# First attention of a two-block kernel: 1/sum carried by a diagonal matrix instead of a scaling pass

## The chip, the cores and the metric
The program runs on one NeuronCore of a Trainium2 chip. Its engines work side by side, each through its own list of instructions in order: PE (TensorE, matrix products), DVE (VectorE), ACT (ScalarE), POOL (GpSimd) and SP (which only issues transfers here). They wait for one another through semaphores. The metric is the device time of one execution in microseconds (us); lower is better.

## The reference
Two transformer blocks run one after the other over 256 tokens of width 1024, in float32. The first has an attention (8 query heads of 64, 2 key/value heads, 512 keys: 256 of a context and 256 of the tokens) and beside it a gated linear recurrence; the second has two further attentions and an MLP. The change touches the first attention alone:

```
def latent_attention(qx, kx, vx, kc, vc):
    ...
    scale = ATT_HEAD_DIM ** -0.5
    def block(q):
        s = jnp.einsum('bqkgd,bnkd->bkgqn', q, keys).astype(jnp.float32) * scale
        p = jax.nn.softmax(s, axis=-1)
        return jnp.einsum('bkgqn,bnkd->bqkgd', p.astype(vals.dtype), vals)
```

with q = rope(rmsnorm(q) * g_q) and k = rope(rmsnorm(k) * g_k). Softmax is exp(s - max) divided by its sum over the 512 keys.

## The kernel before, in words
Nothing is scheduled by a planner: each engine's list is written out by hand, and the order in the source is the order on the engine. `Steps` counts what an engine has finished under a name; `tick` raises the count, `done` raises it and makes DVE wait for it, and `wait_ge(..., DV["probs 3"])` makes another engine wait for that step.

The first attention is cut into 16 units n (8 heads x 2 blocks of 128 queries). Each unit has five steps:

- PE `scores n`: one matmul, 64 x 128 queries against 512 keys, into bank n % 2.
- DVE `max n`: a maximum over the 512 scores (L1227), and a tiny operation that multiplies it by -1/8 (L1228). The result is the bias of the exponential.
- ACT `exp n` (L744): exp(score/8 + bias) from the bank into `probs`, with the row sum beside it.
- DVE `probs n`: the reciprocal of the sum (L1209) and a multiplication of all 512 columns by it (L1210).
- PE `pT n` (L1659): four 128x128 transposes of `probs` into bank 2 + n % 2; ACT copies them out (L736). For every second unit PE then multiplies the transposed probabilities of a head (two units) by the values: `values h`, four matmuls.

The orders around it. PE: `scores n+1`, a piece of the recurrence (`hg_tail n`), `pT n`, and after even n from 2 on `values n/2-1`. The tails are 8 transposes at n = 1, 8 matmuls at n = 2 and 3, 16 matmuls at n = 4 and 5 (8 each in float32 of 256 columns), one of 512 columns at n = 7 and 8, and 8 one-column matmuls at n = 9; n = 6 and 10 to 15 have none. DVE: `probs n-1`, `max n`, then `acc`, a multiply-add over 1024 columns that reduces the modulation weights and has nothing to do with the attention (L1096), and at n = 11 `hg_out`, a block of five operations that finishes the recurrence (L1217 to L1221). ACT: `exp n`, the copy of `pT n-1`, its own tails; at n = 8 these hold a table load, a logarithm and the load back before `exp 9`. From n = 13 ACT also makes the high halves of the next weights, and POOL the low halves (L558).

After unit 15 PE does `values 7`, a reduction (`mod 3`), and then the output projection, which runs back to back.

Of the kernel before, what the change touches and what calls it, by code (L numbers as in the profile page):

```python
# [24 lines left out]
ALU = mybir.AluOpType  # L25
ACT = mybir.ActivationFunctionType
AX = mybir.AxisListType.X

P = 128
# [3 lines left out]
HD = 64  # L33
# [63 lines left out]
class Steps:  # L97
# [8 lines left out]
    def tick(self, name):  # L106
        assert name not in self.seen, name
        self.seen.append(name)
        self.n += 1
        if self.order is not None:  # L110
            assert self.order[self.n - 1] == name, (name, self.order[self.n - 1])
        return 1
# [7 lines left out]
def program(nc, a, out, orders):  # L120

    ctx = ExitStack()
    with ctx:
# [6 lines left out]
        ps = [ctx.enter_context(nc.psum_tensor(f"bank{i}", [P, 512], F32)) for i in range(8)]  # L130
# [11 lines left out]
        stat = sb("stat", [P, 256])  # L142
# [4 lines left out]
        dg = sb("rstd_diag", [P, 2, P])  # L147
        rby = sb("rstd_b", [P, T])
        ident = cst[:, C_ID:C_ID + P]
# [17 lines left out]
        kv = sb("kv", [P, 4, 256], F32, b1)  # L167
        qk = sb("q_k", [P, 2, 640], F32, b1)
        gqk = sb("g_qk_b", [P, 640], F32, b1)
# [31 lines left out]
        pr = sb("probs", [P, 2, 512], F32, r)  # L201
# [154 lines left out]
        PE, AC, DV, PL = (Steps(sem(f"{n}_step"), orders and orders[n]) for n in ("pe", "act", "dve", "pool"))  # L356
# [255 lines left out]
        def _(act):  # L612
# [31 lines left out]
            for t in range(4):  # L644
                src = x[:, t, :] if t < 2 else cx[:, t - 2, :]
                if t:
                    act.wait_ge(AC.sem, AC[f"sq {t - 1}"])
                nc.scalar.activation(junk, src, ACT.Square,
                                     accum_out=stat[:, 64 + t:65 + t]).then_inc(AC.sem, AC.tick(f"sq {t}"))
# [90 lines left out]
            for n in range(16):  # L740
                act.wait_ge(DV.sem, DV[f"max {n}"])
                if n >= 2:
                    act.wait_ge(PE.sem, PE[f"pT {n - 2}"])
                nc.scalar.activation(pr[:, n % 2, :], ps[n % 2][:], ACT.Exp, bias=stat[:, 128 + n:129 + n],  # L744
                                     scale=HD ** -0.5, accum_out=stat[:, 144 + n:145 + n]).then_inc(AC.sem, AC.tick(f"exp {n}"))
                if n >= 1:
                    probs_by_key(n - 1)
                hg_tail(n)
                if n >= 13:
                    hi(W_END["g"] + n - 12)  # L750
# [34 lines left out]
            with act.Fori(0, MLP1_TRIPS) as i:  # L785
                for v in range(2):
                    g = 1 + v
# [94 lines left out]
            for n in range(17):  # L882
                if n < 16:
                    scale = HD ** -0.5 if n < 8 else 96 ** -0.5
# [3 lines left out]
                    for t, (c0, c1) in enumerate(((0, P), (P, 384))):  # L888
                        nc.scalar.activation(pc[:, n % 2, c0:c1], ps[n % 2][:, c0:c1], ACT.Exp, bias=stat[:, 128 + 2 * n + t:129 + 2 * n + t],
                                             scale=scale, accum_out=stat[:, 160 + 2 * n + t:161 + 2 * n + t]  # L890
                                             ).then_inc(AC.sem, AC.tick(f"cexp {n} {t}"))
                if n % 4 == 3:
                    g = n // 4
# [84 lines left out]
        def _(dve):  # L978
            V = nc.vector
# [5 lines left out]
            def tick(ins, name):  # L985
                ins.then_inc(DV.sem, DV.tick(name))

            def done(ins, name):
                ins.then_inc(DV.sem, DV.tick(name))
                dve.wait_ge(DV.sem, DV[name])  # L990
# [162 lines left out]
            for l, n in enumerate(LEVELS):  # L1153
                for i in range(2):
                    dve.wait_ge(PE.sem, PE[f"level {l} {i}"])
                    own(f"at diag {i}" if l == 0 else f"at {l - 1} {i}")
                    mask = cst[:, C_LVL + P * l:C_LVL + P * l + P].bitcast(U32).unsqueeze(1).broadcast_to([P, HG, P])
                    tick(V.copy_predicated(at[:, i, :, P * i:P * i + P], mask,
                                           ps[6 + i][:].rearrange("p (h t) -> p h t", h=HG)), f"at {l} {i}")
                grow(n)  # L1160
                if n == 4:

                    dve.wait_ge(AC.sem, AC["kv 1"])
                    tick(V.tensor_copy(qk[:, :, 512:640], kv[:, 0:2, 0:P]), "k in")
                if n == 16:

                    dve.wait_ge(AC.sem, AC["q 1"])
                    own("k in")
                    V.tensor_tensor(tmp2[:, :, 0:P], kv[:, 2:4, 0:P], kv[:, 2:4, 0:P], ALU.mult)
                    done(V.tensor_tensor(tmp[:], qk[:], qk[:], ALU.mult), "qk sq")  # L1170
                    V.tensor_reduce(stat[:, 80:100].rearrange("p (t h) -> p t h", t=2), tmp[:].rearrange("p t (h d) -> p t h d", d=HD), AX, ALU.add)
                    tick(V.tensor_reduce(stat[:, 100:104].rearrange("p (t h) -> p t h", t=2),
                                         tmp2[:, :, 0:P].rearrange("p t (h d) -> p t h d", d=HD), AX, ALU.add), "qk ss")
                if n == 32:
                    dve.wait_ge(AC.sem, AC["rstd qk"])
                    dve.wait_ge(s_bc, 160)
                    qk4 = qk[:].rearrange("p t (h d) -> p t h d", d=HD)
                    kc4 = kv[:, 2:4, 0:P].rearrange("p t (h d) -> p t h d", d=HD)
                    V.tensor_tensor(qk4, qk4, stat[:, 104:124].rearrange("p (t h) -> p t h", t=2).unsqueeze(3).broadcast_to([P, 2, 10, HD]), ALU.mult)
                    done(V.tensor_tensor(kc4, kc4, stat[:, 124:128].rearrange("p (t h) -> p t h", t=2).unsqueeze(3).broadcast_to([P, 2, 2, HD]), ALU.mult), "qk n")  # L1180
                    V.tensor_tensor(kv[:, 2:4, 0:P], kv[:, 2:4, 0:P], gqk[:, 512:640].unsqueeze(1).broadcast_to([P, 2, P]), ALU.mult)
                    done(V.tensor_tensor(qk[:], qk[:], gqk[:].unsqueeze(1).broadcast_to([P, 2, 640]), ALU.mult), "qk g")
                if n == 64:

                    for t in range(2):
                        c4 = cst[:, C_COS + HD * t:C_COS + HD * t + HD].unsqueeze(1).broadcast_to([P, 10, HD])
                        V.tensor_tensor(tmp[:, t, :].rearrange("p (h d) -> p h d", d=HD), qk4[:, t], c4, ALU.mult)
                        x5 = qk[:, t, :].rearrange("p (h a two i) -> p h a two i", a=2, two=2, i=16)
                        o5 = tmp2[:, t, :].rearrange("p (h a two i) -> p h a two i", a=2, two=2, i=16)
                        s5 = cst[:, C_SIN + HD * t:C_SIN + HD * t + HD].rearrange("p (a two i) -> p a two i", a=2, two=2)  # L1190
                        for half in range(2):
                            ins = V.tensor_tensor(o5[:, :, :, half, :], x5[:, :, :, 1 - half, :],
                                                  s5[:, :, half, :].unsqueeze(1).broadcast_to([P, 10, 2, 16]), ALU.mult)
                    done(ins, "rope")
                    done(V.tensor_tensor(qk[:], tmp[:], tmp2[:], ALU.add), "qk")
# [11 lines left out]
            def probs(n):  # L1207
                dve.wait_ge(AC.sem, AC[f"exp {n}"])
                done(V.reciprocal(stat[:, 160 + n:161 + n], stat[:, 144 + n:145 + n]), f"sum {n}")  # L1209
                tick(V.tensor_scalar(pr[:, n % 2, :], pr[:, n % 2, :], stat[:, 160 + n:161 + n], None, ALU.mult), f"probs {n}")  # L1210

            def hg_out():

# [7 lines left out]
                tick(V.tensor_tensor(flat(cl, 4, 4), xn[:, 1, :], flat(ch, 4, 4).bitcast(F32), ALU.subtract), "cat lo")  # L1221

            for n in range(16):
                if n >= 1:
                    probs(n - 1)
                dve.wait_ge(PE.sem, PE[f"scores {n}"])
                done(V.tensor_reduce(stat[:, 128 + n:129 + n], ps[n % 2][:], AX, ALU.max), f"m {n}")  # L1227
                done(V.tensor_scalar(stat[:, 128 + n:129 + n], stat[:, 128 + n:129 + n], -HD ** -0.5, None, ALU.mult), f"max {n}")  # L1228
                acc(2 + n // KT, n % KT)
                if n == 11:  # L1230
                    hg_out()
                if n == 10:

                    dve.wait_ge(PE.sem, PE["mod 2"])
                    done(V.tensor_tensor(mod2[:, 8:16], ps[5][:, 0:8], cols[:, R_BMOD + 32:R_BMOD + 40], ALU.add), "mod2 s")
                    tick(V.scalar_tensor_tensor(out=mod2[:, 8:16], in0=mod2[:, 8:16], scalar=1.0, in1=cols[:, R_G2:R_G2 + 8],
                                                op0=ALU.add, op1=ALU.mult), "mod2 scale")
# [215 lines left out]
        def _(pe):  # L1453
            def mm(out_, l, r_, start, stop=True):
                return nc.tensor.matmul(out_, l, r_, start=start, stop=stop, skip_group_check=True)  # L1455
# [196 lines left out]
            def probs_t(n):  # L1652
                pe.wait_ge(DV.sem, DV[f"probs {n}"])
                if n >= 2:
                    pe.wait_ge(AC.sem, AC[f"pT {n - 2}"])
                else:
                    pe.wait_ge(AC.sem, AC["qT 2"])
                for k in range(4):
                    ins = nc.tensor.transpose(ps[2 + n % 2][:, P * k:P * k + P], pr[:, n % 2, P * k:P * k + P], ident)  # L1659
                ins.then_inc(PE.sem, PE.tick(f"pT {n}"))  # L1660

            def values(h):
# [364 lines left out]
```

## Time and profile before

| | us |
|---|---|
| median of 3 executions | 999.83 |
| the three executions | 995.11, 999.83, 1000.09 |
| span of the profiled execution (first to last instruction) | 991.5 |
| the profiled execution's own time | not listed apart from the three |
| PE busy | 891.4 (90%) |
| DVE busy | 464.1 (47%) |
| ACT busy | 409.5 (41%) |
| POOL busy | 461.2 (47%) |
| mean granted clock of TensorE | 0.941 of full |

The units of the attention lie between 237 and 316 us of the span. A row of the timeline gives start, length, engine, line, operation, output and inputs, and in brackets the idle time of the engine before it and what ended that. Matmuls overlap in the record, so what one costs is read from its start to the start of the next, not from its length. A float32 matmul leaves two records, a transpose one: "x16" under a matmul of the recurrence is 8 matmuls, "x4" under L1659 is 4 transposes. A granted clock of 1.00 is 2.4 GHz and 0.50 is 1.2 GHz.

### The profile page before, as it was taken

How to read it: one execution, taken by the hardware profiler on the slowest of the kernel's cores; microseconds unless marked ns; L12 is line 12 of the kernel's file. 1: busy time of each engine (PE TensorE's matmuls, PEld its weight loads, DVE VectorE, ACT ScalarE, POOL GpSimd, SP SyncE). 2: the span in 40 equal slices, each digit the busy share in tenths (PEclk: the TensorE clock that was granted, in tenths of full speed). 3: DMA queues.
4: the chain of work that ended last, by engine and by line, in shares of the span. 5: the costliest groups of instructions: out<-in, count | busy, mean ns of one | idle time of the engine just before them, and what ended most of it. 6: DMA issues, size and time to landing. Idle time of an engine off the chain costs nothing.

```text
span 991.5 us, 13660 instructions
## 1 busy us (share of the span) xinstructions
PE 891.4 (90%) x5233; PEld 740.5 (75%) x5233; DVE 464.1 (47%) x642; ACT 409.5 (41%) x627; POOL 461.2 (47%) x225
## 2 busy tenths in 40 slices
PE   5599997997988889999999699999998599999995
PEld 0157797786644669999998587877797489999994
DVE  0259856698574262333333605353325643334334
ACT  1232321215353443444435464544473534444443
POOL 4053634310003616474756398543375356564653
PEclk9799997899977989999999699999999789999998
DMA  9957841221344416656564277432344335666541
GB/s 198 270 198 237 278 122 45 84 64 52 104 121 150 128 64 181 201 170 196 172 201 137 82 217 178 141 86 85 107 137 140 106 89 189 190 189 191 178 161 42
DMA packets 89290, 145.76 MB, mean 147 GB/s; under 512 B 15260, under 2 KB 55297, under 8 KB 89249
## 3 DMA queue, kind: packets, MB, share of 16 engines
q1 hardware_dynamic: 88112, 143.23, 46.6%
q0 software_dynamic: 1104, 1.96, 1.8%
q8 instruction: 27, 0.44, 0.2%
q14 instruction: 15, 0.11, 0.0%
q10 hardware_dynamic: 32, 0.01, 0.0%
HBM read 144.13 MB, written 1.05 MB: 146 GB/s over the span
## 4 chain that ended last, share of the span: by engine, by line
PE 73%; DVE 13%; issue 5%; ACT 3%; DMA 3%; POOL 2%; SPq 0%; DVEq 0%; ACTq 0%; POOLq 0%
PE bank L1455 71%; DMA raw<-in_w_mod 3%; POOL w_lo L558 1%; ACT w_hi L620 1%; DVE hg_kb L1149 1%; DVE hg_b L1151 1%; DVE mod_acc L1096 1%; POOL z_lo L594 1%; PE bank L1659 1%; PE bank L1935 1%; DVE probs L1210 1%; DVE hg_kf L1149 1%; DVE yn L1419 1%; DVE merged_lo L1406 1%; DVE hg_f L1151 0%
## 5 line engine op out<-in xcount | busy, mean ns | idle before, releaser
L558 POOL TENSOR_TENSOR w_lo<-raw,w_hi 128x1024 fp32r<-128x1024 f32 (+2 forms) x177 | 431.6, 2451 | 488.3 <-ACT w_hi L620 446.4
L620 ACT ACTIVATE w_hi<-raw 128x1024 fp32r<-128x1024 f32 (+1 forms) x218 | 227.3, 1044 | 258.0 <-PE bank L1455 243.5
L1455 PE MATMUL bank<-z_hi,w_hi 128*128 128x256 f32 x384 | 111.8, 291 | 2.4 <-POOL z_lo L594 2.4
L1455 PE MATMUL bank<-z_lo,w_hi 128*128 128x256 f32 x384 | 110.3, 287 | 0.0
L1455 PE MATMUL bank<-z_hi,w_lo 128*128 128x256 f32 x384 | 110.1, 287 | 0.0
L1007 DVE TENSOR_TENSOR w_lo<-raw,w_hi 128x1024 fp32r<-128x1024 f32 x44 | 57.4, 1315 | 112.6 <-ACT w_hi L620 112.6
L1455 PE MATMUL bank<-n_hi,w_hi 128*128 128x256 f32 x352 | 100.8, 286 | 1.4 <-DVE w_lo L1007 0.5
L1455 PE MATMUL bank<-n_lo,w_hi 128*128 128x256 f32 x352 | 99.9, 284 | 0.0
L1455 PE MATMUL bank<-n_hi,w_lo 128*128 128x256 f32 x352 | 99.8, 284 | 0.0
L1455 PE MATMUL bank<-w_hi,mlp_h_hi 128*128 128x512 f32 x216 | 84.9, 393 | 3.0 <-DVE mlp_h_lo L1441 1.5
L1455 PE MATMUL bank<-w_lo,mlp_h_hi 128*128 128x512 f32 x216 | 84.7, 392 | 0.0
L1455 PE MATMUL bank<-w_hi,mlp_h_lo 128*128 128x512 f32 x216 | 84.5, 391 | 0.0
L1455 PEld LDWEIGHTS bank<-z_hi,w_hi 128*128 128x128 f32 x384 | 75.3, 196 | 5.2 <-issue 3.1
L1455 PEld LDWEIGHTS bank<-z_lo,w_hi 128*128 128x128 f32 x384 | 75.4, 196 | 0.6
L1455 PEld LDWEIGHTS bank<-z_hi,w_lo 128*128 128x128 f32 x384 | 75.3, 196 | 0.0
L1455 PEld LDWEIGHTS bank<-n_hi,w_hi 128*128 128x128 f32 x352 | 67.2, 191 | 3.6 <-POOL w_lo L558 1.3
L1455 PEld LDWEIGHTS bank<-n_lo,w_hi 128*128 128x128 f32 x352 | 67.3, 191 | 0.4
L1455 PEld LDWEIGHTS bank<-n_hi,w_lo 128*128 128x128 f32 x352 | 67.1, 191 | 0.0
L1455 PEld LDWEIGHTS bank<-w_hi,mlp_h_hi 128*128 128x128 f32 x216 | 40.7, 188 | 11.8 <-DVE mlp_h_lo L1441 1.9
L1439 DVE TENSOR_TENSOR mlp_h<-mlp_relu 128x512 f32<-128x512 f32 x16 | 11.1, 693 | 81.4 <-ACT mlp_relu L958 81.4
L1455 PE MATMUL bank<-raw,c_silu 128*2 128x512 f32 x64 | 32.3, 658 | 17.7 <-DMA raw<-in_w_mod 17.7
L1455 PEld LDWEIGHTS bank<-w_hi,mlp_h_lo 128*128 128x128 f32 x216 | 40.6, 188 | 8.9
(355 smaller groups left out, 1783.3 us busy)
## 6 DMA issues: line engine op xcount, KB each, us to landing
raw<-in_w_in SPq DMA_DIRECT2D x54, 512.0 KB, 4.3
raw<-in_w_down SPq DMA_DIRECT2D x54, 512.0 KB, 3.6
raw<-in_w_mod SPq DMA_DIRECT2D x48, 512.0 KB, 4.3
raw<-in_w_gu SPq DMA_DIRECT2D x44, 512.0 KB, 3.5
raw<-in_w_up SPq DMA_DIRECT2D x32, 512.0 KB, 3.6
raw<-in_w_out SPq DMA_DIRECT2D x12, 512.0 KB, 3.6
raw<-in_w_in SPq DMA_DIRECT2D x8, 336.0 KB, 3.0
raw<-in_w_out SPq DMA_DIRECT2D x8, 256.0 KB, 3.7
```

The costliest lines, as they stand in the source:

```text
L558: nc.gpsimd.tensor_tensor(wl[:, w % SPL, 0:size], raw[:, slot_raw, 0:size], wh[:, w % SPL, 0:size].bitcast(F32), ALU.subtract).then_inc(s_ ...
L594: nc.gpsimd.tensor_tensor(zl[:, k, :], zf[:, k % 4, :], zh[:, k, :].bitcast(F32), ALU.subtract).then_inc(PL.sem, PL.tick(f"{name}l {k}"))
L620: nc.scalar.activation(wh[:, w % SPL, 0:size], raw[:, slot_raw, 0:size], ACT.Copy).then_inc(s_hi, 1)
L1007: V.tensor_tensor(wl[:, w % SPL, :], raw[:, slot_raw, :], wh[:, w % SPL, :].bitcast(F32), ALU.subtract).then_inc(s_lod, 1)
L1096: ins = V.scalar_tensor_tensor(out=to, in0=raw[:, n % RAW, :], scalar=csil[:, k, 0:1], in1=to, op0=ALU.mult, op1=ALU.add)
L1149: ins = V.tensor_tensor(kv_[:, :, 1 - fwd, :], kv_[:, :, 1 - fwd, :], tot(fwd), ALU.mult)
L1151: done(V.tensor_tensor(fv[:, :, 0, 0:1], fv[:, :, 0, 0:1], fv[:, :, 1, 0:1], ALU.mult), f"total {n} {fwd}")
L1210: tick(V.tensor_scalar(pr[:, n % 2, :], pr[:, n % 2, :], stat[:, 160 + n:161 + n], None, ALU.mult), f"probs {n}")
L1406: tick(V.tensor_tensor(flat(mgl, k0, n), flat(mgf, k0, n), flat(mgh, k0, n).bitcast(F32), ALU.subtract), f"merged lo {b}")
L1419: ins = V.scalar_tensor_tensor(out=yn[:, t, 512 * j:512 * j + 512], in0=ps[bank + 2 * t + j][:], scalar=stat[:, 216 + t:217 + t], in1=gpos ...
L1439: V.tensor_tensor(h2[:, g % 3, :], rr[:, g % 3, :], rr[:, g % 3, :], ALU.mult).then_inc(s_h2, 1)
L1455: return nc.tensor.matmul(out_, l, r_, start=start, stop=stop, skip_group_check=True)
```

## The change
The division by the row sum is no longer a pass over the probabilities. DVE multiplies the 128x128 identity by the reciprocal, which gives a diagonal matrix in `dg` (128 columns instead of 512), and PE's four transposes become four ordinary float32 matmuls of `probs` with that diagonal: they transpose and scale at once. The factor 1/8 moves from the exponential and the maximum into g_q: the gain multiplication of queries and keys is split in two, and the one of the queries has the factor in it. The maximum is written negated by the reduction itself, so that L1228 goes, and DVE no longer waits for its own result there. Last, on DVE `max n` now stands ahead of `probs n-1`.

```
-                                     scale=HD ** -0.5, accum_out=stat[:, 144 + n:145 + n]).then_inc(AC.sem, AC.tick(f"exp {n}"))
+                                     accum_out=stat[:, 144 + n:145 + n]).then_inc(AC.sem, AC.tick(f"exp {n}"))
...
-                    V.tensor_tensor(kv[:, 2:4, 0:P], kv[:, 2:4, 0:P], gqk[:, 512:640].unsqueeze(1).broadcast_to([P, 2, P]), ALU.mult)
-                    done(V.tensor_tensor(qk[:], qk[:], gqk[:].unsqueeze(1).broadcast_to([P, 2, 640]), ALU.mult), "qk g")
+                    kg = gqk[:, 512:640].unsqueeze(1).broadcast_to([P, 2, P])
+                    V.tensor_tensor(kv[:, 2:4, 0:P], kv[:, 2:4, 0:P], kg, ALU.mult)
+                    V.tensor_tensor(qk[:, :, 512:640], qk[:, :, 512:640], kg, ALU.mult)
+                    done(V.scalar_tensor_tensor(out=qk[:, :, 0:512], in0=qk[:, :, 0:512], scalar=HD ** -0.5,
+                                                in1=gqk[:, 0:512].unsqueeze(1).broadcast_to([P, 2, 512]),
+                                                op0=ALU.mult, op1=ALU.mult), "qk g")
...
-                tick(V.tensor_scalar(pr[:, n % 2, :], pr[:, n % 2, :], stat[:, 160 + n:161 + n], None, ALU.mult), f"probs {n}")
+                tick(V.tensor_scalar(dg[:, n % 2, :], ident, stat[:, 160 + n:161 + n], None, ALU.mult), f"probs {n}")
...
             for n in range(16):
+                dve.wait_ge(PE.sem, PE[f"scores {n}"])
+                tick(V.tensor_reduce(stat[:, 128 + n:129 + n], ps[n % 2][:], AX, ALU.max, negate=True), f"max {n}")
                 if n >= 1:
                     probs(n - 1)
-                dve.wait_ge(PE.sem, PE[f"scores {n}"])
-                done(V.tensor_reduce(stat[:, 128 + n:129 + n], ps[n % 2][:], AX, ALU.max), f"m {n}")
-                done(V.tensor_scalar(stat[:, 128 + n:129 + n], stat[:, 128 + n:129 + n], -HD ** -0.5, None, ALU.mult), f"max {n}")
                 acc(2 + n // KT, n % KT)
...
-                    ins = nc.tensor.transpose(ps[2 + n % 2][:, P * k:P * k + P], pr[:, n % 2, P * k:P * k + P], ident)
+                    ins = mm(ps[2 + n % 2][:, P * k:P * k + P], pr[:, n % 2, P * k:P * k + P], dg[:, n % 2, :], True)
```

DVE's list at the start of units 13 and 14, before. The reciprocal and `probs` (L1209, L1210) of the last unit come first, then the maximum of this one:

```order
L1209 RECIPROCAL stat<-stat 128x1 [waits act_step]
L1210 TENSOR_SCALAR probs<-probs,stat 128x512 [waits dve_step]
L1227 TENSOR_REDUCE stat<-bank 128x1 [waits pe_step]
L1228 TENSOR_SCALAR stat<-stat 128x1 [waits dve_step]
L1096 SCALAR_TENSOR_TENSOR mod_acc<-raw,c_silu,mod_acc 128x1024 [waits acc_used,raw_full5,dve_step]
L1209 RECIPROCAL stat<-stat 128x1 [waits act_step]
L1210 TENSOR_SCALAR probs<-probs,stat 128x512 [waits dve_step]
L1227 TENSOR_REDUCE stat<-bank 128x1 [waits pe_step]
L1228 TENSOR_SCALAR stat<-stat 128x1 [waits dve_step]
```

The same place after the change (`rstd_diag` is the name of `dg`; the lines are 4 higher, or 2 for the maximum):

```order
L1229 TENSOR_REDUCE stat<-bank 128x1 [waits pe_step]
L1213 RECIPROCAL stat<-stat 128x1 [waits act_step]
L1214 TENSOR_SCALAR rstd_diag<-cst,stat 128x128 [waits dve_step]
L1096 SCALAR_TENSOR_TENSOR mod_acc<-raw,c_silu,mod_acc 128x1024 [waits acc_used,raw_full5]
L1229 TENSOR_REDUCE stat<-bank 128x1 [waits pe_step]
L1213 RECIPROCAL stat<-stat 128x1 [waits act_step]
L1214 TENSOR_SCALAR rstd_diag<-cst,stat 128x128 [waits dve_step]
```

The maximum, which waits for PE, has moved ahead of the reciprocal and the diagonal of the unit before; four operations are left where there were five.

PE's list at units 10 to 12, before: `scores n+1` (keysT,qT), then the transposes of unit n, then in even units the values:

```order
L1455 MATMUL bank<-keysT,qT 128x512 [waits act_step]
L1659 MATMUL bank<-cst,probs 128x128 [waits act_step,dve_step]
L1659 MATMUL bank<-cst,probs 128x128 x3
L1455 MATMUL bank<-probsT,kv 64x256 [waits dve_step,act_step]
L1455 MATMUL bank<-probsT,kv 64x256 x3
L1455 MATMUL bank<-keysT,qT 128x512 [waits act_step]
L1659 MATMUL bank<-cst,probs 128x128 [waits act_step,dve_step]
```

And after:

```order
L1458 MATMUL bank<-keysT,qT 128x512 [waits act_step]
L1458 MATMUL bank<-rstd_diag,probs 128x128 [waits act_step,dve_step]
L1458 MATMUL bank<-rstd_diag,probs 128x128 x3
L1458 MATMUL bank<-probsT,kv 64x256 [waits dve_step,act_step]
L1458 MATMUL bank<-probsT,kv 64x256 x3
L1458 MATMUL bank<-keysT,qT 128x512 [waits act_step]
L1458 MATMUL bank<-rstd_diag,probs 128x128 [waits act_step,dve_step]
```

Nothing has moved on PE; the four transposes have become four matmuls with the diagonal. ACT's list is the same.

## Rows read from the trace of the kernel before

**Rows 1.** The page, the chain that ended last: shares of the span by engine.

```profile
PE 73%; DVE 13%; issue 5%; ACT 3%; DMA 3%; POOL 2%; SPq 0%; DVEq 0%; ACTq 0%; POOLq 0%
```

**Rows 2.** Stretches: from:to, length, busy time of each engine (records), PE clock, DMA.

```profile
237.00:270.00 33.00, 29.90 (x135) 19.59 (x136) 19.63 (x39) 13.22 (x30) 0.00 (x0) 0.95 0.38 112
270.00:282.00 12.00, 11.28 (x50) 5.97 (x48) 6.46 (x14) 8.51 (x15) 0.00 (x0) 1.00 0.46 133
282.00:316.00 34.00, 26.67 (x71) 12.64 (x72) 24.22 (x38) 12.73 (x25) 7.84 (x4) 0.67 0.50 152
```

**Rows 3.** Timeline of PE in unit 3 (start, length, line, tiles).

```profile
252.08 2.05 PE L1455 MATMUL bank<-hg_v,hg_k_tok 128*128 128x128 f32 x16
253.97 0.60 PE L1659 MATMUL bank<-cst,probs 128*128 128x128 f32 x4
254.50 1.12 PE L1455 MATMUL bank<-keysT,qT 64*128 64x512 f32 x2
```

**Rows 4.** Timeline of PE in units 5 to 7.

```profile
266.12 0.60 PE L1659 MATMUL bank<-cst,probs 128*128 128x128 f32 x4
266.65 1.12 PE L1455 MATMUL bank<-keysT,qT 64*128 64x512 f32 x2
268.84 0.66 PE L1659 MATMUL bank<-cst,probs 128*128 128x128 f32 x4 [1.07 <-DVE probs L1210]
269.43 1.94 PE L1455 MATMUL bank<-probsT,kv 128*64 128x256 f32 x8
271.30 1.12 PE L1455 MATMUL bank<-keysT,qT 64*128 64x512 f32 x2
272.35 1.12 PE L1455 MATMUL bank<-xn,cst 128*128 128x512 f32 x2
273.32 0.60 PE L1659 MATMUL bank<-cst,probs 128*128 128x128 f32 x4
```

**Rows 5.** Timeline of PE in units 9 to 15.

```profile
281.99 0.66 PE L1659 MATMUL bank<-cst,probs 128*128 128x128 f32 x4 [0.72 <-DVE probs L1210]
...
286.01 3.67 PE L1455 MATMUL bank<-probsT,kv 128*64 128x256 f32 x8
...
292.12 0.66 PE L1659 MATMUL bank<-cst,probs 128*128 128x128 f32 x4 [1.14 <-DVE probs L1210]
...
294.82 1.11 PE L1659 MATMUL bank<-cst,probs 128*128 128x128 f32 x4 [0.86 <-DVE probs L1210]
295.87 3.68 PE L1455 MATMUL bank<-probsT,kv 128*64 128x256 f32 x8
...
300.96 0.66 PE L1659 MATMUL bank<-cst,probs 128*128 128x128 f32 x4
...
304.20 1.12 PE L1659 MATMUL bank<-cst,probs 128*128 128x128 f32 x4 [1.53 <-DVE probs L1210]
...
310.24 0.80 PE L1659 MATMUL bank<-cst,probs 128*128 128x128 f32 x4 [2.10 <-DVE probs L1210]
```

**Rows 6.** Timeline of DVE in units 9 to 15.

```profile
281.24 0.16 DVE L1209 RECIPROCAL stat<-stat 128x1 f32<-128x1 f32 x1 [3.64 <-ACT probs L744]
...
286.93 1.28 DVE L1217 TENSOR_TENSOR xn<-bank,xn 128x512 f32<-128x512 f32 x2
...
301.07 0.69 DVE L1227 TENSOR_REDUCE stat<-bank 128x1 f32<-128x512 f32 x1 [3.60 <-PE bank L1455]
...
302.26 1.28 DVE L1096 SCALAR_TENSOR_TENSOR mod_acc<-raw,c_silu,mod_acc 128x1024 f32<-128x1024 f32 x1 [0.31 <-DVE stat L1228]
...
307.81 2.37 DVE L1210 TENSOR_SCALAR probs<-probs,stat 128x512 f32<-128x512 f32 x1
```

**Rows 7.** Timeline of POOL at unit 15.

```profile
307.25 2.65 POOL L558 TENSOR_TENSOR w_lo<-raw,w_hi 128x1024 fp32r<-128x1024 f32 x1 [0.63 <-ACT w_hi L620]
```

**Rows 8.** Single lines: ns min/median/max, starts, forms.

```profile
L1309 DVE TENSOR_SCALAR rstd_diag<-cst,stat x4: 285/286/2183, 558.2 to 788.2; 128x128 f32<-128x128 f32 x4
```

**Rows 9.** Single line of the gain multiplication.

```profile
L1182 DVE TENSOR_TENSOR q_k<-q_k,g_qk_b x1: 1483/1483/1483, 218.6 to 218.6; 128x1280 f32<-128x1280 f32 x1
```

## The prediction

> **What bounds the kernel now.** I read the chain that ended last first: PE holds 73% of the span [rows 1], so what counts is what makes PE start late or work longer. The stretches come next [rows 2]. From 237 to 270 us PE is busy 29.90 of 33 us and from 270 to 282 us 11.28 of 12; DVE is busy about half of both. From 282 to 316 us PE is busy 26.67 of 34, its clock is 0.67 in the mean, and DVE is busy 24.22. So the attention has two parts: up to unit 9 PE is full, because the tails of the recurrence stand between `scores n+1` and `pT n` and hide everything that DVE does; from unit 10 there are no tails, and PE waits for DVE in each unit.
>
> The PE timeline shows it. In unit 3 the transposes follow the tail with no idle time [rows 3]. In unit 6, which has no tail, they start 1.07 us late [rows 4]. In units 9, 11, 12, 14 and 15 they wait 0.72, 1.14, 0.86, 1.53 and 2.10 us [rows 5], each time for `probs`. But DVE in turn waits for PE: its maximum of unit 14 comes after 3.60 us of idleness [rows 6]. Neither has slack to give away there.
>
> **Prices.** Four transposes take 254.50 - 253.97 = 0.53 us on PE; the 8 float32 matmuls of the same shape ahead of them take 253.97 - 252.08 = 1.89, so four take 0.94 [rows 3]. A unit's transposition costs 0.41 us more at full clock. At half clock both double: four transposes take 1.05 (295.87 - 294.82) and the values' row is 3.68 long against 1.94 [rows 4, 5]; I take 1.9 for four matmuls, 0.85 more. The two records per matmul are in both numbers. `scores` takes 272.35 - 271.30 = 1.05, the one-matmul tail 273.32 - 272.35 = 0.97, `values` 271.30 - 269.43 = 1.87 [rows 4]. The diagonal is an operation that the trace has elsewhere: 0.29 us [rows 8], against 0.49 for the pass over 512 columns (the worst of both, 2.18 and 2.37, I come to below). The reduction takes 0.69, the reciprocal 0.16, `acc` 1.28 [rows 6].
>
> The TensorE page of the Trainium skill (TensorE: Matmul & The Clock Gate, Terms) says that the transpose mode is 4 times faster for float32. Our rows say 0.94/0.53 = 1.8 times; the rows have both operations at this very shape.
>
> **The new order is a new wait.** Now `max n+1` stands ahead of `probs n` on DVE. It waits for `scores n+1`, which PE issues just ahead of `pT n`. So PE, having finished `scores n+1`, has to see on DVE the reduction (0.69), the reciprocal (0.16) and the diagonal (0.29), with about 0.12 for the hand-overs: 1.26 us between the end of `scores n+1` and the start of `pT n`, in every unit. Before, `probs n` could be ready by then. Behind the waiting `max` on DVE stand the diagonal and `acc`; behind the waiting `pT` on PE stand the values and the next scores. A tail of 1.26 us or more hides it: units 1 to 5 do. Unit 7 has 0.97, units 6 and 10 to 14 nothing, unit 15 has no `max` ahead of it.
>
> **The sum, by stretch** (delay of PE against the profile before).
> - Gains of queries and keys: one multiplication of 1280 elements (1.48 us, [rows 9]) becomes one of 256 and one scalar-tensor-tensor of 1024, whose like is `acc` with 1.28 [rows 6]. The short one is between 0.16 and 0.49. This is 0.0 to 0.3 more; I take 0.1.
> - Unit 0: the diagonal comes behind `max 1`, but is shorter, and L1228 goes. Between -0.2 and +0.7 (one reduction); I take 0.2.
> - Units 0 to 4, PE full: 4 x 0.41, and unit 1 at half clock (the stretch's 0.95 is one short spell there) 0.85: 2.5.
> - Units 5 and 6. Before, `pT 6` starts 268.84 - 266.12 = 2.72 after the last tail ended (bound by ACT). Now: `pT 5` 0.94 + scores 1.05 + 1.26 = 3.25. So 0.5.
> - `pT 6` 0.41, the rest of the new wait in unit 7 (1.26 - 0.97 = 0.29), `pT 7` 0.41: 1.1.
> - Units 8 and 9: the chain runs through ACT (logarithm and two table loads), seen as the 3.64 us that the reciprocal of unit 9 waits [rows 6]. It hides `pT 8`, and the diagonal is 0.2 shorter: -0.2.
> - From `pT 9` to `pT 11`: 292.12 - 281.99 = 10.13 before, set by `hg_out` on DVE, which starts at 286.93 (4.94 in). Now, counted from `pT 9`: matmuls 0.94, scores 1.05, wait 1.26 (`pT 10` at 3.25), `acc` about 1.3, `hg_out` begins at about 4.6, ends 4.5 later, and then `max 12` and the wait: 10.3 if PE is ready. At half clock PE isn't: `pT 10` 1.9, values 3.6, scores 1.3 or more, wait 1.26 give 11.3 to 11.9. Before, the clock was low here (3.67 for the values, [rows 5]). 0.2 to 1.8; I take 1.0.
> - `pT 11` to `pT 13`: 8.84 before. The start of `pT 12` goes from 2.70 to 0.94 + 1.05 + 1.26 = 3.25 (0.55); `pT 12` at half clock 0.85; `pT 13`, which followed its scores at once (300.96, no idle time, [rows 5]), now waits 1.26. That is 2.7; the values come 1.4 us later and so a bit more of them at the higher clock: 2.1.
> - `pT 13` to `pT 14`: 3.24 before, 3.25 now: 0.
> - `pT 14` to `pT 15`: 6.04 before, because the pass of unit 15 took 2.37 us beside POOL's 2.65 us at 307.25 [rows 6, 7]. PE's own work there is 1.9 + 3.6 = 5.5 at half clock. Between -1.2 and, if a diagonal meets POOL (the 2183 ns of [rows 8] is such a one), +1.9: I take -0.6. `pT 15` itself 0.4.
>
> Together 0.1 + 0.2 + 2.5 + 0.5 + 1.1 - 0.2 + 1.0 + 2.1 + 0 - 0.6 + 0.4 = 7.1 us. After 316 us PE runs back to back through the output projection, so the delay is passed on to the end. The span goes from 991.5 to 998.6. The timed runs lie 3.6 to 8.6 us above that span (995.11 to 1000.09); on the median of 999.83 the forecast is **1006.9**.
>
> **Rivals.**
> 1. *The clock stays up.* PE gets real matmuls where it had transposes, and works more. In 282 to 316 us a mean of 0.67 means that some 22 of 34 us ran at half clock; PE's busy share there makes some 17 us of work, of which full clock would give back up to 8.5. Then 999.8 + 7.1 - 8.5 = 998.4, within the noise. For it: the stretch is cold. Against: the clock was 1.00 through the transposes of 270 to 282 us [rows 2], and it is idleness that comes before each drop; the change takes little of that away and adds some (unit 13). The skill has a rule for this rival: the same page (Part 4: PE-mode transpose) says that transposes don't count as busy for the clock. By the rule alone the mean clock of 282 to 316 us should rise clearly.
> 2. *DVE decides, and the change makes it faster.* Each unit loses 0.2 of the pass and 0.2 of L1228; if PE in truth waits for the sum of DVE's work and not for its order, 16 x 0.4 = 6.4 us go, and with the matmuls hidden in the waits the time is 993.4. It decides where DVE has no idle time. For it: PE's waits in rows 5 are all put down to DVE. Against: DVE idles 3.60 us in front of a maximum, and PE is full up to unit 9.
> 3. *Only the matmuls cost.* The new wait is covered by the late `probs` that PE waited for anyway; 3.0 for the full part and about 1 for the rest: 1003.8.
> 4. *The collisions pile up.* A diagonal meets POOL's low halves (+1.9), and the clock drops once or twice in the full part because of the 1.26 us gap in unit 6 (half of a 3.5 us spell each, 1.7 to 3.4): 1011 to 1013.
> 5. *Matmuls are much dearer than the rows say.* By the page's factor of 4, four would take 2.1 us; 1.6 x 14 units on the path = 22 us, 1022. [Rows 3] speaks against it outright.
>
> **Chances.** Forecast 0.52, rival 1 0.17, rival 2 0.08, rival 3 0.12, rival 4 0.10, rival 5 0.01. Within 0.5% of 999.83 (994.8 to 1004.8) a measurement of this kernel can't tell from no change. Rival 2 is faster, 1 and 3 are within, 4, 5 and most of the forecast slower; the forecast's own range is 1003 to 1010, so a part of it falls within. Faster 0.08, same 0.34, slower 0.58. The range takes in rivals 1, 3 and most of 4: 998 to 1013.
>
> **What the profile after would show.** PE's rows of `probs` with the diagonal have two records per matmul, about 0.94 us per four. In units 10 to 14 each such row has about 1.2 us idle before it, put down to the diagonal; that of unit 13 is new. DVE's busy time in 282 to 316 falls by some 4 us while its idle time in front of the maximum grows. ACT's exponentials start earlier, to no use. If the gaps in units 10 to 14 are not there, the order costs nothing and rival 3 holds; if the clock of the stretch is above 0.8, rival 1.

## The result, and the profile after

The changed kernel takes 1004.16 us in the median of 12 executions (1000.99 to 1007.59), the kernel before 999.17 (12 executions, 995.11 to 1004.06): ratio 1.0048, interval 1.0030 to 1.0066. Run once more, word for word, it gave 1.0056 (1.0033 to 1.0080). It is some 5 us slower. Forecast were 1006.9, and slower. The median lies inside the band that the prediction called no change (994.8 to 1004.8); it is told apart from no change only because each kernel has 12 executions, and the interval leaves out 1.

The stretches of the profile after, with the same edges as [rows 2] (from:to, length, busy time of PE, weight loads, DVE, ACT, POOL; clock; DMA):

```profile
237.00:270.00 33.00, 30.02 (x141) 20.42 (x139) 14.44 (x26) 13.74 (x29) 0.00 (x0) 0.84 0.32 96
270.00:282.00 12.00, 10.82 (x47) 6.88 (x46) 5.33 (x11) 3.61 (x8) 0.00 (x0) 1.00 0.30 88
282.00:316.00 34.00, 26.94 (x113) 15.29 (x112) 21.03 (x36) 17.71 (x31) 4.12 (x2) 0.86 0.39 109
```

DVE is busy less than before in all three. The edges are not the same work, since everything comes later. So from here on the attention is cut by events: from its first scores to the reduction behind `values 7`. That is 237.39 to 315.32 before, 77.93 us; 240.45 to 324.92 after, 84.47 us:

```profile
237.39:315.32 77.93, 67.16 (x252) 37.70 (x252) 50.27 (x88) 33.56 (x66) 7.84 (x4) 0.84 0.44 131
240.45:324.92 84.47, 73.67 (x317) 46.33 (x317) 41.80 (x72) 34.32 (x66) 7.53 (x4) 0.86 0.38 114
```

Cut like this, PE is busy 6.5 us more and DVE 8.5 us less: work has moved from DVE to PE. The start of the first scores hardly tells of the change: a second profile of the kernel before, identical, has its first scores at 241.82, and one of the kernel after at 237.48.

PE in units 3, 5 and 6, the answer to [rows 3, 4] (start, length, operation, idle time before):

```profile
260.66 1.06 PE L1458 MATMUL bank<-rstd_diag,probs 128*128 128x128 f32 x8
261.64 1.12 PE L1458 MATMUL bank<-keysT,qT 64*128 64x512 f32 x2
...
273.72 1.05 PE L1458 MATMUL bank<-rstd_diag,probs 128*128 128x128 f32 x8
274.70 1.12 PE L1458 MATMUL bank<-keysT,qT 64*128 64x512 f32 x2
277.00 1.16 PE L1458 MATMUL bank<-rstd_diag,probs 128*128 128x128 f32 x8 [1.18 <-DVE rstd_diag L1214]
```

The four matmuls have two records each (x8) and take 0.98 us from start to start, where four transposes took 0.53. Where PE had to wait for them (unit 6) they take 1.09 to the next start, against 0.59 before. In unit 6 they start 3.28 us after those of unit 5; the forecast was 3.25.

PE in units 11 to 15, the answer to [rows 5]:

```profile
302.72 1.16 PE L1458 MATMUL bank<-rstd_diag,probs 128*128 128x128 f32 x8 [1.18 <-DVE rstd_diag L1214]
...
306.11 1.16 PE L1458 MATMUL bank<-rstd_diag,probs 128*128 128x128 f32 x8 [1.18 <-DVE rstd_diag L1214]
307.20 1.94 PE L1458 MATMUL bank<-probsT,kv 128*64 128x256 f32 x8
...
311.40 1.16 PE L1458 MATMUL bank<-rstd_diag,probs 128*128 128x128 f32 x8 [1.21 <-DVE rstd_diag L1214]
...
316.69 2.08 PE L1458 MATMUL bank<-rstd_diag,probs 128*128 128x128 f32 x8 [2.78 <-DVE rstd_diag L1214]
...
321.20 1.16 PE L1458 MATMUL bank<-rstd_diag,probs 128*128 128x128 f32 x8
```

The gap of units 6 and 10 to 12 is always the same, 1.18 us; unit 13, which had none before, now has 1.21. In these units a wait whose length varied (0 to 1.14 us) has become a fixed one. Unit 14 waits 2.78 us, for the reason below, and unit 15, which waited 2.10 us before, waits no more: no maximum stands ahead of its diagonal.

DVE at the same time (the maximum of unit 14 with the reciprocal and the diagonal of unit 13, then the diagonal of unit 14), the answer to [rows 6]:

```profile
310.23 0.69 DVE L1229 TENSOR_REDUCE stat<-bank 128x1 f32<-128x512 f32 x1 [2.98 <-PE bank L1458]
310.84 0.15 DVE L1213 RECIPROCAL stat<-stat 128x1 f32<-128x1 f32 x1
311.03 0.32 DVE L1214 TENSOR_SCALAR rstd_diag<-cst,stat 128x128 f32<-128x128 f32 x1
...
314.75 1.89 DVE L1214 TENSOR_SCALAR rstd_diag<-cst,stat 128x128 f32<-128x128 f32 x1
```

The maximum of unit 14 waits for PE, and 1.17 us after its start PE is released: each engine waits for the other in turn. The diagonal of 314.75 takes 1.89 us in place of 0.29. POOL is at work beside it:

```profile
314.22 2.34 POOL L558 TENSOR_TENSOR w_lo<-raw,w_hi 128x1024 fp32r<-128x1024 f32 x1 [2.95 <-ACT w_hi L620]
```

It is what the pass of unit 15 met before [rows 6, 7], now in unit 14.

### The profile page after: what moved, and what is told of

It is laid out like the page before. It is cut to its first block, busy times and chain, and to the rows that moved or that the text cites. A ratio compares the mean times of both kernels' runs of the same rounds, so it can differ in the third digit from the quotient of the medians.

```text
span 1003.9 us, 13771 instructions
## 1 busy us (share of the span) xinstructions
PE 907.3 (90%) x5297; PEld 756.2 (75%) x5297; DVE 456.6 (45%) x627; ACT 410.0 (41%) x627; POOL 460.0 (46%) x225
## 4 chain that ended last, share of the span: by engine, by line
PE 78%; DVE 12%; DMA 3%; ACT 3%; issue 2%; POOL 2%; SPq 0%; DVEq 0%; ACTq 0%
PE bank L1458 77%; DMA raw<-in_w_mod 3%; ACT w_hi L620 1%; POOL w_lo L558 1%; DVE hg_b L1151 1%; DVE hg_kb L1149 1%; POOL z_lo L594 1%; DVE stat L999 1%; DVE stat L1229 1%; PE bank L1938 1%; DVE yn L1422 1%; DVE hg_f L1151 1%; DVE x L1428 0%; DVE merged_lo L1409 0%; DVE hg_kf L1149 0%
```

## The experiments

Times are medians; each ratio is against the kernel before, run on the same chip, with its 95% interval. Differences from the kernel before are worked out from the ratio, not from the two medians. "Attention" is the stretch of 77.93 us from a single profile; where a kernel was profiled twice, both are given. Which execution was profiled matters: those of e1, e2 (first) and e10 were the slowest of their twelve, that of e9 (second) the fastest. The kernel before: 77.93 and 79.02. The changed kernel: 84.47 and 83.94.

| run | DVE's order | on PE | ratio | attention, us |
|---|---|---|---|---|
| before | old | transposes | 1 | 77.9, 79.0 |
| e1 | new | transposes | 1.0051 (1.0030 to 1.0071) | 85.9 |
| e5 (negated maximum) | old | transposes | 0.9977 (0.9949 to 1.0005) | 80.0 |
| after | new | matmuls | 1.0048 (1.0030 to 1.0066) | 84.5, 83.9 |
| e2 | old | matmuls | 0.9955 (0.9926 to 0.9983), again 0.9979 (0.9955 to 1.0003) | 81.1, 78.0 |
| e3 (not scaled) | new | transposes | 1.0008 (0.9985 to 1.0030) | 80.5 |
| e9 (not scaled) | old | transposes | 0.9919 (0.9896 to 0.9942), again 0.9939 (0.9917 to 0.9960) | 73.2, 71.7 |
| e4, values early | new | matmuls | 1.0040 (1.0014 to 1.0067) | 84.0 |
| e8, values early | old | matmuls | 0.9995 (0.9965 to 1.0025) | 83.0 |
| e10, transposes twice (not scaled) | new | transposes | 1.0033 (1.0012 to 1.0054) | 85.8 |

**e1: the kernel before with the new order alone.**

```
             for n in range(16):
+                dve.wait_ge(PE.sem, PE[f"scores {n}"])
+                done(V.tensor_reduce(...), f"m {n}")
+                done(V.tensor_scalar(...), f"max {n}")
                 if n >= 1:
                     probs(n - 1)
-                dve.wait_ge(PE.sem, PE[f"scores {n}"])
...
```

> The kernel before with one edit: on DVE, max n stands ahead of the reciprocal and scaling pass of unit n-1. Transposes, pass and the separate negation stay. Theory W (the order makes a new wait: PE has to see reduction, negation, reciprocal and pass after scores n+1): 0.69 + 0.19 + 0.16 + 0.49 and hand-overs = 1.6 us idle ahead of the transposes of units 6, 10 to 14, part of it in unit 7; slower than before by 3 to 5 us, and the attention (first scores to the reduction behind values 7, 77.9 us before) grows to 81 to 83. Theory M (only the dearer matmuls cost, the order is free): within 1 us of before.

1003.41 us, by the ratio of 1.0051 5.1 us slower. In its profile units 11 to 13 read:

```profile
302.94 0.66 PE L1659 MATMUL bank<-cst,probs 128*128 128x128 f32 x4 [1.70 <-DVE probs L1210]
...
307.03 1.11 PE L1659 MATMUL bank<-cst,probs 128*128 128x128 f32 x4 [1.69 <-DVE probs L1210]
...
314.02 1.09 PE L1659 MATMUL bank<-cst,probs 128*128 128x128 f32 x4 [1.69 <-DVE probs L1210]
```

The gap is 1.69 us, against 1.6 worked out. The order alone costs as much as the whole change. Theory M falls. The attention grew even more than theory W said (85.9 against 81 to 83), but the profile is that of the slowest execution (1007.08 us).

**e2: the changed kernel with the old order.**

```
             for n in range(16):
-                dve.wait_ge(PE.sem, PE[f"scores {n}"])
-                tick(V.tensor_reduce(...), f"max {n}")
                 if n >= 1:
                     probs(n - 1)
+                dve.wait_ge(PE.sem, PE[f"scores {n}"])
+                tick(V.tensor_reduce(...), f"max {n}")
```

> The changed kernel with DVE's old order (reciprocal and diagonal of unit n-1 first, then max n); everything else stays changed. Theory W: the 1.18 us gaps of units 10 to 14 go or shrink where DVE is ready, the matmuls (0.41 us dearer per unit at full clock) remain: 0 to 2.5 us slower than before, 2.5 to 4.5 faster than the changed kernel. Theory M: no better than the changed kernel, 4 to 5 us slower than before.

995.68 us: 8.5 us faster than the changed kernel by the medians (9.3 by the ratios) and 4.5 faster than before (0.9955). Theory W had the direction but not the size; it had said that this version can't beat the kernel before. Because that was a surprise, it was run again:

> The diagonal kernel with DVE's old order once more, word for word, for its times on another day of runs and a second profile. Theory W with a diagonal that pays: again 3 to 6 us faster than before. If its first ratio of 0.9955 was luck: within 2 us of before.

996.59 us against 998.52, ratio 0.9979 (0.9955 to 1.0003). The two intervals overlap around 0.997; a gain of about 3 us is the fair reading, less than the first run gave, and the second alone would not have shown it. PE in units 13 and 14 of the second profile:

```profile
306.00 1.16 PE L1458 MATMUL bank<-rstd_diag,probs 128*128 128x128 f32 x8
307.09 1.12 PE L1458 MATMUL bank<-keysT,qT 64*128 64x512 f32 x2
308.44 1.16 PE L1458 MATMUL bank<-rstd_diag,probs 128*128 128x128 f32 x8 [0.23 <-DVE rstd_diag L1214]
```

From one to the next it is 2.44 us, where the changed kernel needs 3.39 in units 11 and 12 (302.72 to 306.11); in its first profile e2 needs 2.18 for those two (302.05 to 304.23). The old order doesn't remove every wait: unit 11 still waits for `hg_out`, 1.15 us in the first profile and 2.55 in the second, and unit 15 for a diagonal beside POOL, 2.92 and 1.06. Where the short gap comes from is seen in unit 10 of the second profile. DVE makes the diagonal first and then the maximum of the next unit, and PE starts beside that maximum:

```profile
289.67 0.29 DVE L1214 TENSOR_SCALAR rstd_diag<-cst,stat 128x128 f32<-128x128 f32 x1
289.88 0.68 DVE L1231 TENSOR_REDUCE stat<-bank 128x1 f32<-128x512 f32 x1
```

```profile
290.01 1.16 PE L1458 MATMUL bank<-rstd_diag,probs 128*128 128x128 f32 x8 [0.25 <-DVE rstd_diag L1214]
```

**e3: the changed kernel, not scaled.** The matmul with the diagonal becomes `nc.tensor.transpose(..., ident)`; nothing else.

> The changed kernel with PE's four matmuls turned back into transposes by the identity; the diagonal is still made and waited for, but not used, so the division by the row sum is left out of the result. Order and waits as changed. Theory W: the 1.18 us gaps stay, PE saves 0.41 us per unit at full clock; 3 to 5 us faster than the changed kernel, about level with before (0 to +2). Theory M: level with before (within 1 us) as well, but with no gaps ahead of the transposes. Theory C (real matmuls hold TensorE's clock up, transposes don't): the mean clock of units 9 to 15 falls from 0.86 in the changed kernel to under 0.75, and the gain is under 2 us.

999.03 us, ratio 1.0008: 4 us faster than the changed kernel and level with before, and the 1.18 us gaps are there. The clock from `pT 9` to the reduction is 0.66:

```profile
283.00:317.09 34.09, 25.63 (x71) 12.13 (x71) 19.89 (x31) 12.82 (x24) 7.54 (x4) 0.66 0.43 126
```

In the changed kernel it is 0.80 in the same stretch (the 0.86 of the expectation is that of 282 to 316 us, which is cut otherwise):

```profile
291.46:324.92 33.46, 25.26 (x101) 14.71 (x100) 19.44 (x31) 12.63 (x24) 7.53 (x4) 0.80 0.43 130
```

The clock did fall, as theory C said, but the gain of 4 us came all the same, as theory W said. It was won in the full part: `pT 9` starts 42.86 us after `pT 0`, against 47.05 and 45.23 in the two profiles of the changed kernel. From `pT 9` to the end they take about the same (34.09 against 33.46 and 35.16).

**e4: the changed kernel with the values ahead of `pT n`.**

```
             for n in range(16):
...
-                probs_t(n)
                 if n >= 2 and n % 2 == 0:
                     values(n // 2 - 1)
+                probs_t(n)
```

> The changed kernel with one edit on PE: in even units the values of the last head stand ahead of pT n instead of behind it, so that 1.87 us of PE work lies in the new wait. Theory W: the gaps of units 6, 10, 12 and 14 go (4 x 1.2 us, unit 14 more), those of 11 and 13 stay; 3 to 5 us faster than the changed kernel, level with before. Theory M: no change (within 1 us).

1004.01 us, ratio 1.0040: nothing gained within the interval. This is a miss for theory W's number; theory M's number fits, but its reason (a free order) fell with e1. PE and DVE in units 11 to 13:

```profile
300.92 1.16 PE L1458 MATMUL bank<-rstd_diag,probs 128*128 128x128 f32 x8 [2.33 <-DVE rstd_diag L1214]
...
303.18 3.46 PE L1458 MATMUL bank<-probsT,kv 128*64 128x256 f32 x8
306.57 1.16 PE L1458 MATMUL bank<-rstd_diag,probs 128*128 128x128 f32 x8
...
311.86 1.16 PE L1458 MATMUL bank<-rstd_diag,probs 128*128 128x128 f32 x8 [3.08 <-DVE rstd_diag L1214]
```

```profile
309.61 2.19 DVE L1214 TENSOR_SCALAR rstd_diag<-cst,stat 128x128 f32<-128x128 f32 x1
```

Unit 12 has no gap any more, as was said. But unit 11 waits 2.33 us instead of 1.18: counted from `pT 9`, PE is ready for it 2.2 us earlier than in the first profile of the changed kernel (7.86 against 10.08 us), while its diagonal, which stands behind `hg_out` on DVE, lets PE start only 1.1 us earlier (10.19 against 11.26). And the diagonal of unit 13 now falls beside POOL and takes 2.19 us, as that of unit 14 did. The filled gaps came back as others.

**e8: the same with the old order.**

> The changed kernel with DVE's old order, and on PE the values ahead of pT n in even units. Theory W (the wait comes from the new order alone): there is no gap for the values to fill, so within 1.5 us of the diagonal kernel with the old order, or up to 2 us slower, since the copies of the transposed block come later. Rival: the values' place matters whatever the order of DVE: 2 us or more faster than it.

1001.81 us, ratio 0.9995 (0.9965 to 1.0025). By the ratio it lies between the kernel before and e2, and gains nothing over e2 whichever of its two runs is taken; the intervals overlap. The rival (the place of the values pays by itself) is refused. Theory W allowed up to 2 us more than e2; by the ratios it is 1.6 to 4.

**e5: the kernel before with the negated maximum.** The edits of the gains, the exponential and L1228 are in, the order, the pass and the transposes stay.

> The kernel before with the negated maximum alone (the reduction writes it negated, the separate negation is gone, the 1/8 in the query gains); pass over 512 columns, transposes and DVE's old order stay. It asks what in the diagonal kernel with the old order made it 4.5 us faster than before. Theory N (the lighter unit on DVE: 0.19 us of negation per unit, on the way from scores to exp): 1 to 2 us faster than before. Theory D (the diagonal does it): within 1 us of before.

999.0 us against 998.52, but the ratio over all runs is 0.9977 (0.9949 to 1.0005): inconclusive, and neither theory is decided. Its twelve times lie in two clumps, three at 989 to 991 and nine at 998 to 1001.

**e9: e2, not scaled** (old order, transposes by the identity, the diagonal made and waited for).

> The changed kernel with DVE's old order and with plain transposes by the identity instead of the matmuls with the diagonal; the diagonal is made and waited for, but not used, so the division by the row sum is left out of the result. Theory P (the matmuls cost what the rows say, 0.41 us more per unit wherever PE is full): 3 to 5 us faster than the diagonal kernel with the old order, some 991. Theory C (real matmuls hold the clock up and pay for themselves): within 1.5 us of it, and the mean clock of units 9 to 15 falls from 0.88 to under 0.75.

990.32 us (6 executions counted, where the others have 12), ratio 0.9919; 5.4 us below the first run of e2. Once more:

> The kernel with DVE's old order, the diagonal made but not used and plain transposes (the division by the row sum is left out of the result), once more. Theory P (matmuls cost 0.41 us more per unit where PE is full): 7 to 9 us faster than before again, 4 to 6 faster than with the matmuls. Theory C (the clock pays for them): it comes back to within 2 us of the version with the matmuls.

992.26 us, ratio 0.9939 (0.9917 to 0.9960). It is 6.1 us faster than before, a little less than the 7 to 9 that were expected. Theory P holds in its direction: by the ratios the matmuls cost 2 to 6 us in the old order, taking each run of e9 against each of e2, some 4 in the mean, and 4 in the new order (e3). The attention takes 73.2 and 71.7 us against 81.1 and 78.0 in e2. The clock from `pT 9` on is 0.71 and 0.78 here, 0.88 in both profiles of e2: again lower, and again it does not eat up the gain.

**e10: e3 with each transpose done twice.** What raises the clock, real matmuls or simply more work for PE?

```
-                for k in range(4):
+                for k in list(range(4)) * 2:
                     ins = nc.tensor.transpose(...)
```

> The changed kernel (new order) with plain transposes in place of the matmuls with the diagonal, and each of the four done twice, so that PE is busy as long as with the four matmuls (8 x 0.13 = 1.06 us against 4 x 0.235 = 0.94 at full clock). The diagonal isn't used, so the division by the row sum is left out of the result. It asks why the clock of units 9 to 15 was 0.80 with the matmuls and 0.66 with transposes. Theory B (it is how long PE is busy): 0.78 or more, and a time within 2 us of the changed kernel. Theory T (transposes count for little or nothing): 0.70 or less, and 2 to 5 us slower than the changed kernel.

1002.31 us, ratio 1.0033. The stretch from `pT 9` to the end:

```profile
294.05:327.07 33.02, 24.51 (x100) 13.87 (x99) 19.81 (x31) 12.69 (x24) 7.54 (x4) 0.84 0.47 133
```

0.84 with eight transposes per unit, against 0.66 with four (e3) and 0.80 and 0.81 with four matmuls; the scores and the values are matmuls in all of them. These are single profiles but for the changed kernel. Two profiles of one kernel differ by at most 0.07 here (e9), so the step from 0.66 to 0.84 is clear. Theory B holds: transposes raise the clock too, if PE has as much to do with them as with the matmuls.

**The two kernels again.** Each was profiled a second time:

> The kernel before, word for word, for a second profile: how much of the difference between two profiles is the execution and not the kernel. Attention stretch (first scores to the reduction behind values 7) again 76 to 80 us, the part ahead of it between 236 and 242 us whatever the kernel.

> The changed kernel, word for word, for a second profile and more times: attention stretch again 83 to 86 us, gaps of 1.18 us ahead of the diagonal matmuls of units 10 to 13, 4 to 6 us slower than before.

The second profile of before has an attention of 79.02 us and its first scores at 241.82 us; the second of after 83.94 and 237.48. The part ahead of the attention thus varies by over 4 us between executions of one kernel, more than most differences here. The attention varies by 1.1 and 0.5 us in these two kernels, by 1.5 in e9 and by 3.1 in e2.

## Why the prediction was right

The direction held, and so did the two costs that it named, the matmuls and the new wait. The sum came near, 7.1 us forecast and 5.0 measured, but in part by luck, as is shown below. The attention of the two kernels differs by 5.7 us in the means of their two profiles. By its own steps, delays in us from the means of both profiles:

| step | forecast | measured |
|---|---|---|
| first scores to `pT 0` | 0.2 | 0.1 |
| `pT 0` to `pT 5` | 2.5 | 2.7 |
| `pT 5` to `pT 6` | 0.5 | 0.6 |
| `pT 6` to `pT 9` | 0.9 | 1.3 |
| `pT 9` to `pT 11` | 1.0 | 1.9 |
| `pT 11` to `pT 13` | 2.1 | -0.1 |
| `pT 13` to `pT 15` | -0.6 | 0.6 |
| `pT 15` to the reduction | 0.4 | -1.4 |

The full part, up to unit 9, came out close to what was worked out from the rows. Its cleanest piece is `pT 2` to `pT 5`, all at full clock: 17.50 and 17.49 us before, 18.86 in both profiles after, so 0.46 us per unit against 0.41. That the whole step to `pT 5` came to 2.7 owes something to luck: it holds a spell at half clock in the first two units, and two profiles of one kernel differ by 1.1 us in it before and by 1.8 after. From `pT 6` to `pT 9` the forecast left out the rest of the new wait in unit 8, 0.27 us like that of unit 7, and that matmuls behind a wait take 1.09 us. The gaps of unit 6 and of units 10 to 13 are 1.18 to 1.21 us, against 1.26. The gains of queries and keys cost what was bounded (the new multiplication of 1024 elements takes 1.22 us, the short one 0.42).

The late part was mis-sized: 2.9 us forecast from `pT 9` on, 1.0 measured. From `pT 11` to `pT 13` the forecast took the half clock of before for granted (values 3.68 us); after, the values of that place take 1.94, at full clock, and that paid for the gap. The same holds for `pT 15` to the reduction, where `values 7` take 1.94 us instead of 3.67. So rival 1 was in part true: the clock from `pT 9` on rose from 0.67 in both profiles to 0.80 and 0.81, and these two steps came out 4.0 us below their forecast. In the window of 282 to 316 us it was 0.86 and 0.82, above the 0.8 by which the prediction would have known rival 1; but that window doesn't hold the same work. Its time (998.4, no change) did not come. Of its two reasons, "PE gets real matmuls where it had transposes, and works more", e10 supports the second: eight transposes do what four matmuls do. The TensorE page of the Trainium skill (TensorE: Matmul & The Clock Gate, Part 4: PE-mode transpose) says that a transpose doesn't count as PE-busy in the same way; e10 disagrees, with 0.84 for eight transposes per unit against 0.66 for four. The row of before, cut like those shown for e3 and the changed kernel:

```profile
281.99:315.32 33.33, 26.00 (x70) 12.15 (x70) 24.23 (x38) 12.17 (x24) 7.84 (x4) 0.67 0.49 148
```

From `pT 13` to `pT 15` the collision with POOL, which was only an end of the range, took place in both profiles (gaps of 2.78 and 3.08 us in unit 14).

The reading of the rows had a slip of no weight: from unit 10 on PE waited "in each unit", but in unit 13 it did not, as the sum itself says further on.

The argument missed one thing, which only the experiments show. It took the change as two costs, the matmuls and the order, with DVE's relief worth almost nothing (-0.6 and -0.2). It is three parts, and the relief is large. The kernel e9 has it and neither cost: 6 to 8 us faster than before. The matmuls take some 4 of that back (e9 to e2), and the order 7 to 9 us in the presence of the diagonal (e2 to after, 0.9955 or 0.9979 against 1.0048; e9 to e3, 0.9919 or 0.9939 against 1.0008), 5 in the kernel before (e1). The forecast's order terms, 0.3 to 1.3 us each in a few units, sum to less than 3. A relief and an order cost that were both too small by about as much cancelled in the sum: that is luck.

Where each part lies is seen when the attention is split at `pT 9`, where the tails of the recurrence end (us; two numbers are two profiles):

| run | `pT 0` to `pT 9` | `pT 9` to the reduction |
|---|---|---|
| before | 41.0, 42.1 | 33.3, 33.3 |
| e9: relief | 41.8, 41.4 | 28.1, 27.1 |
| e2: relief, matmuls | 48.3, 45.8 | 29.5, 28.7 |
| e3: relief, order | 42.9 | 34.1 |
| after: relief, matmuls, order | 47.1, 45.2 | 33.5, 35.2 |

In means, the relief is worth next to nothing in the full part and 5.7 us in the late one. The order costs 5.2 (e2 to after) and 6.5 us (e9 to e3) in the late part, and in the full part -0.9 and 1.3, less than two profiles of e2 differ by. The matmuls cost 5.5 and 3.3 us in the full part, 1.5 and 0.2 in the late one. So each part acts where the prediction's own division of the attention says it should: work on PE where PE is full, DVE's time and order where PE waits. What failed was to put the relief of the late part at 0.6.

The relief's 5.7 us come in two ways. PE waits 3.3 us in units 10 to 15 of e9, where it waited 6.5 before (means of two profiles); units 14 and 15, which waited 1.53 and 2.10, read in the second profile of e9:

```profile
303.56 0.66 PE L1662 MATMUL bank<-cst,probs 128*128 128x128 f32 x4 [0.73 <-DVE rstd_diag L1214]
...
307.64 0.66 PE L1662 MATMUL bank<-cst,probs 128*128 128x128 f32 x4 [1.56 <-DVE rstd_diag L1214]
```

The other 2.5 us are PE's own work, done at a clock of 0.71 and 0.78 instead of 0.67:

```profile
285.58:313.72 28.14, 24.41 (x70) 11.30 (x70) 20.30 (x32) 12.23 (x24) 8.44 (x4) 0.71 0.52 155
284.69:311.79 27.10, 22.81 (x71) 10.65 (x71) 20.12 (x32) 12.24 (x24) 8.43 (x4) 0.78 0.54 161
```

How much of the relief is L1228 and how much the shorter operation is not shown: e5, which has the first alone, takes 31.9 us from `pT 9` on, 1.4 less than before, but that is one profile and its time is inconclusive.

The prediction says that ACT's exponentials start earlier "to no use". That is true only in the new order: there the reciprocal and the diagonal start when the maximum ends, however early the exponential was (310.84 behind 310.23). In e2 the maximum runs beside PE's matmuls.

Rival 2 (faster, 993.4) was wrong for the changed kernel, but its mechanism, DVE's work deciding, is at work from `pT 9` on, as e9 and e2 show once the order is undone. Rival 3 (only the matmuls cost, 1003.8) came nearer to the measured 1004.16 than the forecast did, by luck: the gaps are there, and e1 shows what they cost. Of rival 4 the collision with POOL came true; the clock drop behind the gap of unit 6 is not in the changed kernel (values 1.94 us long) but in e1 and e3 (3.49 and 3.43). Rival 5, a factor of 4 between matmul and transpose, is refused by the row: 0.98 to 0.53.

The version that beats both kernels is e2: the whole change without its reordering, about 3 us faster than before and 8 faster than the changed kernel.

## What to carry to other kernels

An in-order engine that serves two waits should first do the one whose input is there already: putting the operation that waits for PE's newest result ahead of the one that PE needs next turned the latency of both into a gap here, in every iteration that had no other work to cover it, even though no operation was added (e1). Split a change of several edits before judging it: here the diagonal and the lighter maximum were worth 3 us together and the reordering cost 8. When a gap is filled with other work, look at what the next engine was waiting for; e4 filled the gaps of the even units and got them back in the odd ones.

## What the runs showed of the hardware

- Four float32 matmuls of 128x128 cost 0.98 us from start to start, four float32 transposes of the same shape 0.53, at full clock (units 3 and 5, after and before); behind a wait of PE 1.09 and 0.59 (unit 6).
- Transposes hold the clock up too: from `pT 9` on it was 0.66 with four per unit (e3), 0.84 with eight (e10), 0.80 and 0.81 with four matmuls (after), in three kernels with the same order and nearly the same waits.
- An operation of 0.29 us on DVE (a scaling with one input tensor, in SBUF) took 1.89 us (after, 314.75) and 2.19 (e4, 309.61) when it fell beside one of POOL of 2.34; a reduction out of PSUM that lay wholly beside one of POOL kept its 0.69 (e1, 317.15 beside 316.77).
- The times of some kernels fall into clumps some 4 to 5 us apart (first run of e9: 989.9 to 990.4 and 993.8 to 994.2; first of e2: near 990, 996 and 1000), those of others don't (second of e9: 989.1 to 996.5), and profiles of one kernel differ by as much ahead of the changed place, at a mean clock of 0.93 or 0.89 there. For differences of 0.5% a single profile of each kernel can't be subtracted as a whole. Stretches cut by events are steadier, but not exact: the attention of e2 differs by 3.1 us between two profiles, its part from `pT 9` on by 0.8.
